# rstd at the joints of two transformer blocks: square root on ScalarE and reciprocal on VectorE in place of Ln and Exp, with the first tile of h made earlier

## What is computed

```python
def rmsnorm(x, w):
    return x * lax.rsqrt(jnp.mean(x * x, axis=-1, keepdims=True) + EPS) * w

# block 1
h = rmsnorm(x, mix_pre_w) * (1 + sc_m) + sh_m
y = hybrid_mixer(h, ...)                       # w_in, convolution, gated linear attention, w_out
x = x + g_m * rmsnorm(y, mix_post_w)
h = rmsnorm(x, ffn_pre_w) * (1 + sc_f) + sh_f
y = conv_ffn(h, w_up, ffn_conv_w, w_down)
x = x + g_f * rmsnorm(y, ffn_post_w)
# block 2
h = rms_norm(x, norm1_w_2) * (1 + scale1) + shift1
...                                            # w_in_2, pooling, stick-breaking attention, w_o_2
x = x + gate1 * (merged @ w_o_2)
h2 = rms_norm(x, norm2_w_2) * (1 + scale2) + shift2
x = x + gate2 * (square(relu(h2 @ w_ff1_2)) @ w_ff2_2)
```

## Time and profile before

| | |
|---|---|
| median of 3 runs | 2540.71 us (2540.33 to 2541.07) |
| the profiled execution's own time | 2540.95 us |
| its span, first to last instruction | 2539.6 us |
| granted TensorE clock, mean | 0.994 of full |
| TensorE busy | 2476.4 us, 98% of the span |
| VectorE busy | 1995.0 us, 79% |
| ScalarE busy | 1284.4 us, 51% |
| DMA, mean | 257 GB/s |

### The profile page before, as it was taken

How to read it: one execution, slowest core, us unless ns; L and a number is a source line. 1 busy time by engine, 2 the same in 40 slices (tenths; PEclk the granted TensorE clock), 3 DMA queues, 4 the chain that set the end, 5 groups by cost and what they waited for, 6 DMA issues and landing times.

```text
span 2539.6 us, 38354 instructions
## 1 busy us (share of the span) xinstructions
PE 2476.4 (98%) x15324; PEld 2208.6 (87%) x15324; DVE 1995.0 (79%) x2632; ACT 1284.4 (51%) x1877; POOL 4.0 (0%) x11
## 2 busy tenths in 40 slices
PE   6799999999999999999999999999999999999999
PEld 5689999898888888889888888888898888888888
DVE  7889989978977888889976678998678756656655
ACT  5454445555555555555535566554454444444443
POOL 0000000000000000000000000000000000000000
PEclk9999999999999999999999999999999999999999
DMA  9988888667767778777568577888578655555553
GB/s 374 392 326 312 320 315 323 237 231 254 266 247 267 262 251 288 264 255 266 175 247 304 197 253 263 309 318 292 183 253 319 250 190 192 185 194 185 189 193 133
DMA packets 142387, 652.16 MB, mean 257 GB/s; under 512 B 13009, under 2 KB 64209, under 8 KB 77441
## 3 DMA queue, kind: packets, MB, share of 16 engines
q1 hardware_dynamic: 141106, 645.06, 71.0%
q0 software_dynamic: 672, 3.31, 0.3%
q10 hardware_dynamic: 432, 1.35, 0.2%
HBM read 647.58 MB, written 2.10 MB: 256 GB/s over the span
## 4 chain that ended last, share of the span: by engine, by line
PE 82%; DVE 9%; DMA 4%; ACT 2%; issue 2%; DVEq 0%; SPq 0%; ACTq 0%
PE PM L574 44%; PE PM L575 23%; DVE raw L1199 3%; DVE WL L1192 3%; DMA raw<-in_w_in 3%; PE PM L571 2%; PE PM L573 2%; PE PM L572 2%; PE PS L571 2%; PE PS L573 2%; PE PS L572 2%; ACT WH L832 1%; DMA raw<-in_w_mod 0%; PE PS L600 0%; PE PS L602 0%
## 5 line engine op out<-in xcount | busy, mean ns | idle before, releaser
L832 ACT CAST WH<-raw 128x1024 fp32r<-128x1024 f32 (+1 forms) x881 | 882.4, 1010 | 1001.6 <-PE PM L575 676.4
L1192 DVE TENSOR_TENSOR WL<-raw,WH 128x1024 fp32r<-128x1024 f32 (+1 forms) x881 | 1017.7, 1173 | 443.1 <-ACT WH L832 440.8
L574 PE MATMUL PM<-H,WH 128*128 128x512 f32 x2944 | 1032.6, 395 | 0.7 <-DVE WL L1192 0.7
L575 PE MATMUL PM<-H,WL 128*128 128x256 f32 x2944 | 825.3, 280 | 0.0
L574 PEld LDWEIGHTS PM<-H,WH 128*128 128x128 f32 x2944 | 551.8, 187 | 129.1 <-issue 1.2
L575 PEld LDWEIGHTS PM<-H,WL 128*128 128x128 f32 x2944 | 556.2, 189 | 0.3 <-issue 0.2
L1199 DVE CUSTOM_DVE_ANT_0 raw<-raw,cb 128x2048 f32<-128x2048 f32 x192 | 437.1, 2284 | 2.2 <-DMA raw<-in_w_mod 1.0
L574 PE MATMUL PM<-FC,WH 128*128 128x512 f32 x1024 | 358.6, 393 | 0.0
L575 PE MATMUL PM<-FC,WL 128*128 128x256 f32 x1024 | 285.7, 279 | 0.0
L574 PEld LDWEIGHTS PM<-FC,WH 128*128 128x128 f32 x1024 | 191.8, 187 | 45.8
L571 PE MATMUL PM<-H,WH 128*128 128x256 f32 (+1 forms) x656 | 191.4, 292 | 33.2 <-DVE H L1223 30.9
(11 more groups left out here) (313 smaller groups left out, 3119.5 us busy)
## 6 DMA issues: line engine op xcount, KB each, us to landing
raw<-in_w_ff SPq DMA_DIRECT2D x128, 1024.0 KB, 4.9
raw<-in_w_in SPq DMA_DIRECT2D x112, 1024.0 KB, 6.2
raw<-in_w_mod SPq DMA_DIRECT2D x96, 1024.0 KB, 7.2
raw<-in_w_ada SPq DMA_DIRECT2D x96, 1024.0 KB, 6.2
raw<-in_w_up SPq DMA_DIRECT2D x80, 1024.0 KB, 5.2
raw<-in_w_down SPq DMA_DIRECT2D x64, 704.0 KB, 5.5
raw<-in_w_out SPq DMA_DIRECT2D x16, 1024.0 KB, 6.9
raw<-in_w_o SPq DMA_DIRECT2D x16, 1024.0 KB, 6.1
```

Source lines behind the costliest of these rows:

```text
L574: PE.matmul(bank(n)[:, :], wh, rhs, start=(kk == 0), stop=False)
L575: return PE.matmul(bank(n)[:, T:2 * T], wl, rhs[:, 0:T], start=False, stop=ends)
L832: S.copy(part(WH), w).then_inc(s_hi, 1)
L1192: V.tensor_tensor(part(WL), w, part(WH).bitcast(F32), ALU.subtract).then_inc(s_lo, 1)
```

## The change

In `mean_square` the reciprocal of rstd comes first. In `make_h` the tiles are interleaved in another way: ahead of the second reciprocal only tile 0 is gated and added to x, then `scaled(0)` is made, and the work on later tiles follows, one tile less ahead than before. At joint 3 the loop's order stays.

```diff
-            def to_rstd(dst, src):
-                step(S.activation(dst[:, :], src, ACT.Ln, bias=eps[:, 0:1]))
-                S.activation(dst[:, :], dst[:, :], ACT.Exp, scale=-0.5).then_inc(s_rstd, 1)
+            def root(dst, src):
+
+                S.activation(dst[:, :], src, ACT.Sqrt, bias=eps[:, 0:1]).then_inc(s_root, 1)
...
                     S.wait_ge(s_ysum, 2 * use + 1)
-                    to_rstd(rstd, S0)
-                    load_ln()
+                    root(rstd, S0)
                     S.wait_ge(s_u, use + 1)
-                    to_rstd(rstd2, SX[:, :])
+                    root(rstd2, SX[:, :])
...
+            def reciprocal_of(t, count):
+
+                V.wait_ge(s_root, count)
+                V.reciprocal(t[:, :], t[:, :]).then_inc(s_rstd, 1)
+
             def mean_square(use):
 
                 u = tmps[:, 3, :]
+                reciprocal_of(rstd, 2 * use + 2)
                 V.wait_ge(s_ysum, 2 * use + 2)
                 V.wait_ge(s_rstd, 2 * use + 2)
...
-                for i in range(3):
-                    gated(i)
-                    if i:
-                        new_x(i - 1, own[0] - 1)
-                new_x(2, own[0])
+                gated(0)
+                new_x(0, own[0])
                 V.wait_ge(s_eff, (EFF_S1, EFF_S2, EFF_S3)[use])
+                reciprocal_of(rstd2, (3, 5, 6)[use])
                 V.wait_ge(s_rstd, (3, 5, 6)[use])
                 scaled(0)
-                scaled(1)
+                gated(1)
+                new_x(1, own[0])
                 for i in range(16):
-                    if i:
+                    if i or not y_of:
                         scaled(i + 1)
                     V.wait_ge(s_hh, 16 * (use + 1) + i + 1)
                     rest_h(tmps[:, i % 4, :], i)
-                    gated(i + 3)
+                    if y_of and i == 0:
+                        scaled(1)
+                    gated(i + 2)
                     if i + 2 < 16:
                         rest_unit(units[i + 2])
-                    new_x(i + 3, own[0])
+                    new_x(i + 2, own[0])
...
                 mod(0, k)
+                if k == 0:
+                    reciprocal_of(rstd, 1)
```

More of the change, by code:

```diff
@@ L417, in build @@
         s_sq, s_sqadd, s_pre, s_xr, s_at = (sem(x) for x in ("s_sq", "s_sqadd", "s_pre", "s_xr", "s_at"))
+        s_root = sem("s_root")
         s_sqmm, s_ysq, s_yz, s_xz, s_yadd, s_ysum, s_u, s_rstd = (
@@ L838, in low_half, with load_root @@
                 S.copy(low(n), bank(n)[:, T:2 * T]).then_inc(s_low, 1)
-            def load_ln():
-                S.preload_act_table_set("natural_log")
+            def load_root():
+                S.preload_act_table_set("sqrt_and_others")
             def load_logs():
                 S.preload_act_table_set("natural_log_exp_and_others")
-            def to_rstd(dst, src):
-                step(S.activation(dst[:, :], src, ACT.Ln, bias=eps[:, 0:1]))
-                S.activation(dst[:, :], dst[:, :], ACT.Exp, scale=-0.5).then_inc(s_rstd, 1)
+            def root(dst, src):
+                S.activation(dst[:, :], src, ACT.Sqrt, bias=eps[:, 0:1]).then_inc(s_root, 1)
             def round_h(t, i):
@@ L909, in behind @@
                     elif j.i == 2:
-                        load_ln()
+                        load_root()
                     y_squares(0, j.i, acc(n), eff[:, 32 + j.i:33 + j.i])
@@ L994, in gla @@
                 elif h == 63:
-                    load_ln()
+                    S.preload_act_table_set("natural_log")
                     S.wait_ge(s_gpe, PE_NORM)
@@ L1162, in scalar @@
                     S.wait_ge(s_ysum, 5)
-                    to_rstd(rstd2, S0)
+                    root(rstd2, S0)
                     S.wait_ge(s_eff, EFF_S3)
```

## The result

The changed kernel takes 2544.14 us in the median of 20 runs, before takes 2540.29 in 20 runs beside them. The ratio is 1.0015 with a 95% interval of 1.0009 to 1.0022: slower by 0.15%. That is under the 0.2% that the forecast counted as no change, but the interval is clear of one, so these runs can tell it. Forecast were 2544.1 us. The profiled execution takes 2544.80 us, its span is 3.9 us longer than before.

The account below looks back on a forecast made before the run. TensorE, busy 98% of the span, was taken as the bound, moved by its waits at the joints. 5R - 5.61 us with R = 1.8 gave +1.03, +2.27 and +0.09, together +3.4: median 2544.1 us, range 2538.0 to 2549.0.

Parts of the forecast that it names:

- the bound: TensorE works 98% of the span, so a joint counts only for time in which TensorE has no products to run.
- R: Duration of VectorE's reciprocal of 256 columns at the roots: 1.8 us chosen, between 0.42 and 2.28, break-even at 1.12.
- Eight passes: Rival: VectorE's reciprocal runs the columns through eight times, R about 2.3; slower, 2546.5 us, chance 0.27.
- the wait ahead of tile 1: At joints 1 and 2, TensorE waits about 0.19 us once under the new order.
- Sqrt at the duration of Ln: On ScalarE, Sqrt has Ln's shape and operands and was given its 0.47 to 0.51 us.
- no cost of the semaphore: The semaphore s_root costs no instruction of its own on the busy engines.
- the subtractions at joint 2: VectorE's two subtractions had hidden the removed load and Exp almost whole; the first root there gives R - 0.10 us.
- the gap at joint 1: TensorE's gap ahead of the products of zeros at joint 1, 0.33 us before, becomes about 0.8.
- the start at nothing: The start's root shifts by R - 1.63 us, put at nothing: ScalarE's 49.1 us of weight waits before 175 us hide it.
- The clock rivals: TensorE's clock falls at joint 1 or 2: 2.4 us more, 2546.5, chance 0.11; or stays up at joint 3: 2535.1, 0.05.
- a clock that differs at a joint: Sign that the forecast is wrong: TensorE's granted clock differs at a joint; no size given.

Follow-up runs that it names:

- one pass: The changed kernel with the reciprocal replaced by a minimum with 0.01 over the same 256 columns: 2534.61 us, ratio to before 0.9978.
- order alone: The kernel before with Ln and Exp kept and only the new order of tiles in make_h: 2541.44 us, ratio to before 1.0003.
- start undone: The changed kernel with only the root at the start made by Ln and Exp again: 2543.66 us, ratio to before 1.0015.
- units behind: The changed kernel with joint 2's two subtractions moved, one behind SX and one behind scaled(0): 2547.83 us, ratio to before 1.0030.
- the change with zeros: The changed kernel with eight more products of zeros behind joint 3's sums and two more behind its root: 2541.17 us, ratio to before 1.0002.
- the zeros: The kernel before with eight more products of zeros behind joint 3's sums and two more behind its root: 2537.86 us, ratio to before 0.9989.
- two halves: The changed kernel with every reciprocal of 256 columns cut into two of 128: 2543.27 us in a single run.
- the root with the old order: The changed kernel with Sqrt and reciprocal kept, but make_h in the order of before: 2548.16 us, ratio to before 1.0036.

## Why the prediction was right

**Right, and shown:** the bound. All three joints changed by what VectorE and ScalarE do between the sums and `rest_h(0)`, and the sum of removed and added instructions there meets the measured joints to 0.02 us once R is put in. At joint 1 that holds for executions with a half clock just ahead of it, as in the trace that the forecast was read from; in the others VectorE is free earlier, the first reciprocal starts when Sqrt ends, and the change costs 0.44. The change breaks even at R = 1.12 by the forecast; one pass at 0.29 us gives a gain, 1.75 a loss, as that has it.

**Right, with luck in the size:** R. The forecast bounded it between 0.42 and 2.28 us only, and 1.8 was a choice. Both bounds should have stood further out: a pass with one source took 0.29 us, and the longest instruction of VectorE in the trace of before is not the 2.28 but 2.35 us, for 2048 columns (line 1493). Eight passes, the rival that would have made the change slower by over 0.2%, did not come. The rule of the Trainium skill behind it, in VectorE: DVE Perf Modes, "First, the fixed hardware budget", is a repeat count of 8; the measured 6.25 ns a column are six times the 1.05 ns by which a subtraction grows for each column (1222 ns for 1024 columns and 953 for 768 in the groups by shape). The measurement decides.

**Slightly off:** the wait ahead of tile 1, 0.29 us at each of joints 1 and 2 in place of 0.19.

**Right, and not the whole:** Sqrt at the duration of Ln (0.47 and 0.51 us in both), no cost of the semaphore that can be seen, and the subtractions at joint 2 as what had hidden the first root there. That joint alone makes 1.97 of the 3.4 us that the joints and the two waits of 0.29 add up to. What the forecast did not work out is that the gap ahead of the second zeros grows there from 0.30 to 1.94 us; it priced the gap at joint 1 only.

**Agrees, but is not shown to a microsecond:** the start at nothing. The +1.34 at the entry of joint 1 is inside a spread of some 3 us between executions.

**The table switch:** the second rule of the Trainium skill that the forecast weighed, 1.38 us of drain on top of the load (ScalarE: Activation LUTs, "What ACT_TABLE_LOAD costs"), is contradicted again. Where the load between Ln and Exp goes away, joint 3 shrinks by 1.28 us, the load's own duration, and not by 2.66. (Five times 1.38 is 6.9 and not 6.8 us, a slip without effect.)

**The clock rivals:** the clock did fall at joint 2, as one of them had it, in the very execution that was profiled, but it was back before the first product. The forecast had named a clock that differs at a joint as a sign that it was wrong; the sign came, and cost nothing. In four other executions (order alone, start undone, units behind, the change with zeros) it fell just behind joint 1's first product and cost 1.2 us there, not the 2.4 that the rival had taken. Order alone has no reciprocal, so this is not the change's doing alone. The 2.4 were too high at joint 3 as well: at half clock the products there follow each other by 0.21 us in place of 0.12, not by double, and what came back with the zeros is 2.0. That joint 3's idle time brings a half clock is shown by the zeros. How often the unprofiled runs of either kernel had a fall is not known.

What agrees by chance is the total. The forecast's terms make 3.4 us with R = 1.8 and 3.1 with 1.75; the joints and the two waits measured 3.4, 0.2 of it from waits that were put too low. The medians differ by 3.85, with an interval of 2.3 to 5.6, and the base of the forecast, 2540.71, lay 0.4 above the median of 20 runs.

## What to carry to other kernels

Before an operation on ScalarE is traded for one on VectorE, ask which of the two has idle time between its neighbours on the path: here the reciprocal was dearer (1.75 us) than the table load and Exp it replaced (1.70), and at joint 2 the old pair had been hidden and the new instruction was not. When a table load stands between two functions, look first for a table that holds both; here it gained twice what the change lost (7.9 against 3.85 us), 2.6 of it at the joints in the profiled execution, the rest in the attention and behind joint 3. And where the matrix engine must wait between stages, price what the first products behind the wait run at, not only the wait.

## What the runs showed of the hardware

The reciprocal of VectorE costs 6.25 ns a column and 0.15 us fixed, by two widths, against 1.05 ns for a subtraction; two halves in a row take 1.77 us, the whole 1.75. A minimum with a constant over the same 256 columns takes 0.29 us. At joint 3 TensorE's granted clock fell to half (1.2 of 2.4 GHz) when it had been idle for 1.86 us (before) or 2.02 us (change) between its products of zeros there, and stayed up when the gap was 1.3 us shorter or filled with products of zeros. With units behind it came too, later and for a shorter time (722.7 us behind joint 3 in place of 723.4). At joint 2, 1.94 us of idle time ahead of the zeros were followed by a half clock there in the change, start undone and two halves, and not in the change with zeros or the root with the old order: equal gaps, both outcomes. At joint 1, 0.74 and 2.02 us in the profiled execution were not, and in others they were.
